# A network of two blocks: the gated unit by seven block products, and the expert stage's start, order of projections and end rearranged

## The reference

```python
def peer_ffn(h, w_q, sub_keys, u, v):            # first block: x = x + peer_ffn(rmsnorm(x, norm_ffn), ...)
    q = (ht @ w_q).reshape(T, PEER_HEADS, 2, PEER_DKEY // 2)                  # 512 tokens, 8 heads, 2 x 128
    s = jnp.einsum('thpc,hpnc->thpn', q, sub_keys)
    v1, i1 = lax.top_k(s[:, :, 0], K)                                          # K = 16
    v2, i2 = lax.top_k(s[:, :, 1], K)
    cand = (v1[..., :, None] + v2[..., None, :]).reshape(T, PEER_HEADS, K * K)
    cand_idx = (i1[..., :, None] * PEER_NKEYS + i2[..., None, :]).reshape(T, PEER_HEADS, K * K)
    top_s, pos = lax.top_k(cand, K)
    idx = jnp.take_along_axis(cand_idx, pos, axis=-1)
    g = jax.nn.softmax(top_s, axis=-1)
    ue = jnp.take(u, ib, axis=0)                                               # 128 tokens at a time
    a = jnp.einsum('thkd,td->thk', ue, xb)
    w = jax.nn.gelu(a) * gb
    ve = jnp.take(v, ib, axis=0)
    return jnp.einsum('thk,thkd->td', w, ve)

# second block, second mixer: the gated unit behind the state-space layer
    z = jax.nn.gelu(y)
    mix = (z @ w_glu_a) * jax.nn.sigmoid(z @ w_glu_b)
    x = x + gate_m * mix
# second block, second feed-forward
    h = _rmsnorm(x, norm_g[layer, 1]) * (1.0 + scale_f) + shift_f
    x = x + gate_f * (jnp.square(jax.nn.relu(h @ w_fc1[layer])) @ w_fc2[layer])
```

## Time and profile before

| What | Value |
|---|---|
| Runs of the kernel | 3541.75, 3543.51, 3547.22 us |
| Profiled execution, its own time | 3536.91 us |
| Its span, first to last instruction | 3535.1 us |
| Mean granted clock of TensorE | 0.958 |
| PE / DVE / ACT / POOL busy | 89% / 56% / 20% / 19% |
| Moved by DMA | 799.12 MB, of it 619.09 MB on the queue of POOL |
| Expert stage, norm to next stage's norm | 628.77 to 1999.99 us |
| Gated unit, first matmul to last root | 2997.44 to 3117.44 us |

### The profile page before, as it was taken

One profiled execution on the slowest core, in us unless ns is written; L12 is line 12 of the kernel. 1 busy time (PEld: TensorE's weight loads), 2 busy tenths in 40 slices (PEclk: granted clock), 3 DMA queues, 4 the chain that ended last, 5 costly groups with the idle time before them and its releaser, 6 DMA issues. The chain is left out here.

```text
span 3535.1 us, 29320 instructions
## 1 busy us (share of the span) xinstructions
PE 3160.9 (89%) x10728; PEld 1644.0 (47%) x10728; DVE 1973.6 (56%) x4299; ACT 710.6 (20%) x1547; POOL 659.2 (19%) x649
## 2 busy tenths in 40 slices
PE   8999799889888777887877889999999978989998
PEld 3454454334333333333333334534444466468887
DVE  5565831477667777777776319435653366056422
ACT  2133221122222222222221220112110033011000
POOL 0110100144445445444444100000000000000000
PEclk9999899999999999899899999999999999999999
DMA  5653411599999999999999322113453354212222
GB/s 194 240 161 108 155 60 60 220 422 417 417 419 407 421 421 421 421 420 421 409 421 421 155 109 84 48 41 115 159 190 136 120 192 171 71 60 84 84 85 82
DMA packets 118672, 799.12 MB, mean 226 GB/s; under 512 B 13728, under 2 KB 16416, under 8 KB 31872
## 3 DMA queue, kind: packets, MB, share of 16 engines
q0 software_dynamic: 91312, 619.09, 43.6%
q1 hardware_dynamic: 27216, 178.15, 14.1%
HBM read 767.83 MB, written 29.36 MB: 226 GB/s over the span
## 5 line engine op out<-in xcount | busy, mean ns | idle before, releaser
L1278 PE MATMUL po<-pair,diag 128*128 128x512 f32 x2048 | 992.5, 643 | 221.0 <-ACT diag L1338 220.9
L1425 DVE SCALAR_TENSOR_TENSOR pair<-pair,h_tm 128x1024 f32<-128x1024 f32 x512 | 616.7, 1225 | 298.5 <-DMA pair<-in_peer_uv,idx 295.0
L1278 PEld LDWEIGHTS po<-pair,diag 128*128 128x128 f32 x2048 | 411.7, 205 | 781.0 <-issue 489.7
L1198 POOL DMA_INDIRECT pair<-in_peer_uv,idx x512 | 586.8, 1146 | 959.5 <-PE po L1278 663.1
L1571 PE MATMUL acc<-a,ring 128*128 128x512 f32 x512 | 220.9, 592 | 0.0
L1332 ACT ACTIVATE ge<-a 128x4 f32<-128x4 f32 x128 | 26.3, 205 | 896.0 <-DVE pair L1425 896.0
L1556 PE MATMUL acc<-hT,ring 128*128 128x512 f32 x480 | 206.2, 592 | 0.0
L1338 ACT ACTIVATE diag<-ident,wt 128x128 f32<-128x128 f32 x512 | 163.7, 390 | 29.5 <-DVE wt L1428 29.5
L1571 PEld LDWEIGHTS acc<-a,ring 128*128 128x128 f32 x512 | 97.3, 190 | 122.5 <-issue 122.5
L1556 PEld LDWEIGHTS acc<-hT,ring 128*128 128x128 f32 x480 | 91.2, 190 | 114.8 <-issue 114.8
L523 PE MATMUL acc<-hT,first 128*128 128x512 f32 x304 | 136.0, 602 | 5.4 <-ACT mg L707 5.4
(11 more groups left out here) (462 smaller groups left out, 4030.6 us busy)
## 6 DMA issues: line engine op xcount, KB each, us to landing
ring<-in_w_fc SPq DMA_DIRECT2D x62, 1024.0 KB, 4.9
mg<-in_ada_w POOLq DMA_DIRECT2D x96, 512.0 KB, 5.0
s_tables<-table POOLq DMA_DIRECT2D x16, 1664.0 KB, 6.6
tab<-s_tables SPq DMA_DIRECT2D x16, 1664.0 KB, 6.4
ring<-in_w SPq DMA_DIRECT2D x15, 1024.0 KB, 4.8
first<-in_w_first SPq DMA_DIRECT2D x14, 1024.0 KB, 5.1
other<-in_w_first SPq DMA_DIRECT2D x14, 1024.0 KB, 5.0
pair<-in_peer_uv,idx POOLq DMA_INDIRECT x512, 14.7
```

What stands on the lines that cost most here:

```text
L1198: pool.indirect_dma_start(out=pair[:, at, :], out_offset=None, in_=core.dram["peer_uv"][:, :], in_offset=bass.IndirectOffsetOnAxis(ap=idx[ ...
L1278: last = pe.matmul(po[:, t % 2, half * 512:(half + 1) * 512], diag[:, at, :], pair[:, at, D + half * 512:D + (half + 1) * 512], start=firs ...
L1425: dve.scalar_tensor_tensor(row, row, 1.0, h_tm[:, t, :], ALU.mult, ALU.mult, accum_out=a[:, g, s:s + 1]).then_inc(dotted, 1)
```

## The change

- Expert stage, start: the norm runs over the first 128 tokens, then over the other 384. The projections 0 and 1 run over the first 128 tokens (`project_first`), unit 0 is scored and tile 0 turned, then the same projections run over the rest (`project_rest`). Then follow score 1, the projections 2 and 3 and score 2. On ACT the exponentials of the units 0 and 1 stand ahead of the projections 2 and 3. The keys and `iota` are loaded ahead of weight chunk 1.
- Expert stage, middle: twelve projections (4 to 15) in the units 0 to 11 (`LAST_PROJECT` 11), each in two halves behind the gathers 4 and 8 of a unit. Groups of gathers (`groups`): two in the units 0 to 11, four after that, and in the last unit 4, 4, 4, 2, 1, 1. `tokens(1)` in unit 0, `tokens(2)` and `tokens(3)` behind the units 12 and 13. The operations over `hit` run once for both halves of the key, with 512 elements; `cand` and `left` share its memory. ACT copies a tile's output behind the first group of the next unit.
- Expert stage, end: tiles are turned back, added, squared and summed one at a time: 0, 1 and 2 within the units 17 to 31, tile 3 at the end.
- Gated unit: `glu_halves`, with the seven products of `Pairs` for the pairs 1 to 7 and whole products (`Pairs.first`) for pair 0; the weights are laid out for it on the host.
- Last feed-forward: its pairs run through `Pairs` too; pair 0 is made of whole products, which follow the norm tile by tile.

```diff
-LAST_PROJECT = 10
+LAST_PROJECT = 11
...
+def groups(unit):
+
+    if unit <= LAST_PROJECT:
+        return [(s, 2) for s in range(0, PK, 2)]
+    if unit < UNITS - 1:
+        return [(s, GRP) for s in range(0, PK, GRP)]
+    return [(0, 4), (4, 4), (8, 4), (12, 2), (14, 1), (15, 1)]
...
-            sp.dma_start(ring[1], w[P:2 * P, :]).then_inc(w_landed[1], 16)
             sp.dma_start(keys[:, :, :], core.dram["sub_keys"].rearrange("p (h n) -> p h n", n=PN)).then_inc(tables, 16)
             sp.dma_start(iota[:, :], core.const("iota16")).then_inc(tables, 16)
+            sp.dma_start(ring[1], w[P:2 * P, :]).then_inc(w_landed[1], 16)
...
         @block.tensor
...
+            def project_first(i):
+
                 for k in range(KT):
                     if i == 0:
-                        pe.wait_ge(products.ready, k + 1)
+                        pe.wait_ge(normed, k + 1)
+                    last = pe.matmul(acc[:, i, 0:P], ring[0][:, k * 256 + i * P:k * 256 + (i + 1) * P], core.hT[:, k, 0:P],
+                                     start=(k == 0), stop=(k == KT - 1))
+                last.then_inc(first_made, 1)
...
+            pe.wait_ge(core.first_landed, 16 * fetched)
+            project_first(0)
+            project_first(1)
             pe.wait_ge(tables, 32)
             score(0)
+            tokens(0)
+            project_rest(0)
+            project_rest(1)
             score(1)
-            tokens(0)
-            project(2)
-            tokens(1)
-            project(3)
+            for i in range(2, 4):
+                project(i, 0)
+                project(i, 1)
             score(2)
-            tokens(2)
-            tokens(3)
-            project(4)
-            project(5)
...
+                if unit == 2 * PH + 2:
+                    turn_back(1)
+                if unit == 2 * PH + 3:
+                    sum_squares(0)
+                    sum_squares(1)
...
+                    end = s0 + size
+                    if unit <= LAST_PROJECT and end in (4, 8):
+                        project(unit + 4, end // 4 - 1)
+                    if end == 12 and unit + AHEAD + 1 < UNITS:
                         score(unit + AHEAD + 1)
-            turn_back(1)
-            for k in range(KT):
-                sums.add(pe, k)
+                    if end == 12 and unit == 0:
+                        tokens(1)
+                    if end == PK and unit in (LAST_PROJECT + 1, LAST_PROJECT + 2):
+                        tokens(unit - LAST_PROJECT + 1)
+                    if end == 8 and unit == UNITS - 1:
+                        turn_back(2)
+            sum_squares(2)
+            turn_back(3)
+            sum_squares(3)
...
         @block.scalar
...
+            for i in range(2):
+                act.wait_ge(first_made, i + 1)
+                act.activation(qT[:, i, 0:P], acc[:, i, 0:P], ACT.Copy).then_inc(first_taken, 1)
             score(0)
+            tokens(0)
+            for i in range(2):
+                act.wait_ge(made, i + 1)
+                act.activation(qT[:, i, P:S], acc[:, i, P:S], ACT.Copy).then_inc(taken, 1)
+            exponentials(0)
             score(1)
-            tokens(0)
+            exponentials(1)
             project(2)
-            tokens(1)
-            exponentials(0)
             project(3)
             score(2)
...
+                    if end == PK and unit == 0:
+                        tokens(1)
...
-                for q in range(2):
-                    step(dve.tensor_tensor(hit[:, :, :], partf[:, q, :].unsqueeze(2).to_broadcast([P, PK, PK]),
-                                           iota[:, :].unsqueeze(1).to_broadcast([P, PK, PK]), ALU.is_equal))
+                step(dve.tensor_tensor(hit[:, :, :, :], partf[:, :, :].unsqueeze(3).to_broadcast([P, 2, PK, PK]),
+                                       iota[:, :].unsqueeze(1).unsqueeze(1).to_broadcast([P, 2, PK, PK]), ALU.is_equal))
...
+class Pairs:
...
+    def first(self, pe, ready=None):
+        for out, column, done in ((self.x(0), 0, self.x_made), (self.y(0), 1, self.made)):
+            for k in range(KT):
+                if ready is not None and column == 0:
+                    pe.wait_ge(ready, k + 1)
+                last = pe.matmul(out, self.halves.block(0, 2 * column + k // 4)(k % 4), self.h[:, k, :], start=(k == 0), stop=(k == KT - 1))
+            last.then_inc(done, 1)
...
+def glu_halves(core, following):
...
+        @block.scalar
+        def _(act):
+            for p in range(KT):
+                if p >= 2:
+                    act.wait_ge(mixed, p - 1)
+                if p:
+                    pairs.copies(act, p)
+                    pairs.first_quarter(act, p, gate[:, p % 2, LOW], ACT.Sigmoid).then_inc(pairs.c_taken, 1)
+                    act.wait_ge(added, p)
+                    sums.square(act, p - 1)
+                    act.wait_ge(pairs.y_taken, p)
+                    act.activation(gate[:, p % 2, HIGH], gate[:, p % 2, HIGH], ACT.Sigmoid).then_inc(gated, 1)
+                else:
+                    act.wait_ge(pairs.x_made, 1)
+                    act.activation(gate[:, 0, :], pairs.x(0), ACT.Sigmoid).then_inc(pairs.x_copied, 1)
...
```

More of the change, by code:

```diff
@@ new lines, in out @@
+            def out(unit):
+                t = place(unit)[0]
+                act.wait_ge(used, (unit + 1) * PK)
+                for half in range(2):
+                    part = slice(half * 512, (half + 1) * 512)
+                    act.activation(y_tm[:, t, part], po[:, t % 2, part], ACT.Copy).then_inc(tile_out, 1)
+            for i in range(2):
+                act.wait_ge(first_made, i + 1)
+                act.activation(qT[:, i, 0:P], acc[:, i, 0:P], ACT.Copy).then_inc(first_taken, 1)
@@ L1414, in _ @@
                 pick_experts(unit)
+            done = 0
             for unit in range(UNITS):
                 t, h = place(unit)
-                if unit < 2 * AHEAD:
+                if h == 0:
                     dve.wait_ge(copied, 2 * t + 2)
-                for g in range(PK // GRP):
-                    for s in range(GRP):
-                        n = unit * PK + g * GRP + s
+                for s0, size in groups(unit):
+                    for s in range(s0, s0 + size):
+                        n = unit * PK + s
                         at, _, filled = slot[n]
@@ L1646, in sum, with wait, block @@
-    def sum(self, c, i, k):
-        return self.sums[:, c % 2, i - 1, k * P:(k + 1) * P]
-def core_first_or_ring(feed, c):
-    return feed.core.first[:, :] if c == 0 else feed.ring[:, (c - 1) % 2, :]
+    def wait(self, pe, c, n):
+        pe.wait_ge(self.ready, 4 * c - 4 + n)
+    def block(self, c, i):
+        w = self.feed.chunk(None, c, False)
+        return lambda k: w[:, i * 512 + k * P:i * 512 + (k + 1) * P]
+    def sum(self, c, i):
+        return lambda k: self.sums[:, c % 2, i - 1, k * P:(k + 1) * P]
@@ L1751, in _ @@
                     if kk == 0 and j == 0:
[L1752 removed]
+                        pe.wait_ge(pairs.y_taken, HT - 1)
                     if kk == 0 and j:
                         pe.wait_ge(added, 2 * j)
[L1755 removed]
+                    quarter(pe, last_half, halves.block(n, 3), lambda k: t[:, 2, at + k, :], start).then_inc(made, 1)
                     if kk == 1 and j:
```

506 lines of the change are left out of this document (271 added, 235 removed).

## The result

The changed kernel takes 3497.56 us (median of four runs, 3497.26 to 3498.12) against 3542.63 for the kernel before in the same comparison: a ratio of 0.9874, 95% interval 0.9858 to 0.989. The forecast was 3508, range 3501 to 3525. The direction was right; the time lies 3.4 us under the range.

The account below looks back on a forecast made before the run. It took the DMA stream to bound the expert stage and TensorE the gated unit and last feed-forward. Terms summed to -35.2 us on the profiled 3536.9, giving 3501.7; plus 6.6 for the median, 3508, range 3501 to 3525.

Parts of the forecast that it names:

- norm to first gather: Expert stage, start: norming and projecting 128 tokens first brings the first gather earlier, minus 10 us.
- dry gap, block 2: Expert stage, unit 0: no dry stream, minus 8 us; weight block 2 now loads inside the stream, plus 2.5 us.
- after the last landing: Expert stage, end: smaller last groups let TensorE finish sooner behind the last gather, minus 5 us.
- gated unit: Gated unit: seven products of 256 columns per pair in place of 32 instructions of 512, minus 9.8 us.
- first pair of the feed-forward: Last feed-forward, start: whole blocks let TensorE follow each biased tile, minus 4.9 us.
- median above the profiled execution: Whole kernel: the median of the runs lies 6.6 us above the profiled execution, added to the sum.
- Start of the stream: Expert stage, start: scoring 9.5 us earlier, merged `hit` operations 0.5 us less, first gather at about 647.0, minus 10 us.
- The dry gap: Expert stage, unit 0: exponentials of unit 1 ahead of the projections keep the stream from running dry, minus 8 us.
- sums of squares of tile 2 (32 instructions of 128 columns, 4.4): Expert stage, end: TensorE work behind its last weights, 4.4 us within a tail of 14.1 us.
- (D): Rival, gated unit: its pairs wait for copies and sums, 3513 us; chance 0.1.
- (B): Rival, expert stage: the stream still runs dry in unit 0, 3516 us, with the slow start 3521; chance 0.2.
- (E): Rival, units 0 to 11: short bursts let TensorE's clock fall, slower, 3575 us at a clock of 0.75; chance 0.04.

Follow-up runs that it names:

- run 11: The changed kernel with groups of four gathers in units 0 to 11 too, in place of two: 3496.16 us, ratio to before 0.9878.
- run 3: The kernel before with only the exponentials of unit 1 moved ahead of tokens(2), tokens(3) and projection 4: 3540.7 us, ratio to before 1.0005.
- run 6: The kernel before with only projections 4 and 5 moved into the units, exponentials left behind tokens(3): 3534.7 us, ratio to before 0.9992.
- run 8: The changed kernel with the norm and first two projections over all 512 tokens before the first scoring: 3503.31 us, ratio to before 0.9905.
- run 1: The changed kernel with the whole expert stage of the kernel before: 3520.8 us, ratio to before 0.9954.
- run 5: The kernel before with projections 4 and 5 moved into the units and the exponentials of unit 1 moved ahead: 3531.8 us, ratio to before 0.9979.
- Run 7: The changed kernel with each matmul of the new sums of squares issued twice: 3498.7 us, ratio to before 0.9888.
- run 4: The changed kernel with the last unit of the expert stage in groups of four: 3503.3 us, ratio to before 0.9901.
- run 14: The changed kernel with groups of four in units 0 to 11, last tile turned back earlier, last unit 4, 4, 2, 2, 2, 1, 1: 3492.04 us.
- run 12: The changed kernel with the last tile turned back before the squares of tile 2 are summed: 3495.9 us, ratio to before 0.9878.
- run 9: The changed kernel with the last feed-forward of the kernel before: 3501.17 us, ratio to before 0.989.

## Why the prediction was right, and where it was wrong

| term | forecast | trace |
|---|---|---|
| stage before the norm (unchanged code) | 0 | +2.8 |
| norm to first gather | -10 | -11.15 |
| dry gap, block 2 | -8 + 2.5 | -7.06 |
| after the last landing | -5 | -10.25 |
| the stages up to the norm at 2807 (unchanged) | 0 | +0.9 |
| gated unit | -9.8 | -9.1 |
| first pair of the feed-forward | -4.9 | -5.0 |
| sum on the profiled execution | -35.2 | -38.8 |
| median above the profiled execution | +6.6 | -0.6 |

**What bounds it**, the stream: right. The share is 1.01 before and after, and run 11 shows that steps in its shade cost nothing.

**Start of the stream**: right within 1.2 us. The first gather came 17.0 us behind the norm (forecast 18.2), since the 32 short instructions took 5.46 us where I had 6.5, and scoring followed TensorE's last of them after 0.46 us where I had 0.7. The last landing came 15.4 us earlier, as forecast (15 to 16), but in part by luck: the stage before, whose code is unchanged, ended 2.8 us later, and the two terms gave 2.7 us more than forecast.

**The dry gap**: the size was near, the cause wrong. I named the exponentials, because the trace put DVE's 14.87 us on them. They were one of two waits. The other, ACT and TensorE on projections 4 and 5, ended 1.5 us later and holds the slot as long by itself, and it also held up the exponentials. My list by hand had the two projections left in front of unit 0 right and so gave the right result for the wrong line: run 3 moves that line alone and gains nothing, run 6 moves the other and gains the gap. Run 8 confirms the 2.5 of block 2 as 2.6. The gap itself is no fixed number: 7 us of idle stream in the trace that the 8 was read from, 4 in runs 1 and 3, where projections 4 and 5 started 3.4 us sooner. Later in the stream it scatters too: first gather to last landing, the same data took 1308.2 us in run 8 and 1310.5 and 1311.2 in runs 5 and 6, all without a gap. What moves it there was not tried.

**After the last landing**: right in mechanism, wrong in size. TensorE ended 6.3 us behind the last landing, 6.1 were forecast. Of the 4.7 us less than before, 1.7 are the half clock that the first trace of before happened to have there (run 1). The step that failed is "sums of squares of tile 2 (32 instructions of 128 columns, 4.4)" and "32 instructions more 4.5": they are 16 each, 1.95 and 2.05 us. That is 4.9 of the 5.3 us; the copies and hand-overs between give the rest. A tile's sum is eight matmuls, and every matmul of this kernel shows as two instructions; I doubled once too often. Run 7 bears the size out: 32 instructions more cost 3.6 us, 0.11 each, where the forecast had 0.14.

**Gated unit and feed-forward**: right, 13.0 forecast and 12.95 measured for a pair with its sum, 4.9 and 5.0 for the first pair. (D) did not happen. The -9.1 is the difference of two traces; from the norm at 2807 to that of the feed-forward the 11 traces with the new unit take 275.5 to 279.3 us and the four others besides before 285.8 to 288.2.

**The median**: the step "The median of the runs is 6.6 above it" is the largest miss. It took the median of three runs for a property of the kernel, and for one that the change leaves alone. Of 56 runs of before only three were above that median of 3543.51. Whether that was luck or the chip of those runs is open; the changed kernel's four runs beside them lay 0.0 to 0.9 us under their own profiled execution. Against the pooled median, 1.4 us above the profiled execution, the same sum gives 3503.1, and with the sums of squares sized by their rows 3498.2, where the pooled median of after is 3497.9. It took both steps to miss: with either one put right, the lower end of the range would lie at 3496, under the result.

**Rivals.** (B): the share stayed at 1.01 in 673 to 715, and slot 12's gather went out at 705.24 (listed: 703.9). (E): the clock was 0.97 in 700 to 1140. The rule of the Trainium skill that spoke for it (TensorE: Matmul & The Clock Gate, HAM oscillation) does not take hold here: TensorE's bursts there are on the whole not shorter than its waits, since it is busy for 392.80 of 440 us.

## What to carry to other kernels

A wait that the trace puts down to one instruction may hide a second that ends at about the same time, and may itself be held up by it: before pricing its removal, list what the waiting chain needs next and when that is ready. Count the instructions of a short step from the rows of its like, not from the loop: here one factor of two was worth as much as a whole term. And with three runs that spread over 5 us, sum and result are best both held against a profiled execution, or against a median of many runs.

## What the hardware showed that I had not expected

Much of the scatter between the profiled executions is the placing of short spells at half clock. From the norm at 2356 to the one at 2807 (times of the changed kernel) the code is unchanged. In the 16 profiled executions of this study that stretch took 450.8 us six times, 452.5 six times and 453.6 or 453.7 four times, and each time the granted clock of its first 15 us or so tells which: never under full speed, half clock for 3.4 us, half clock for 6.8 us. Here are the changed kernel (450.8), run 8 (452.5) and run 4 (453.7), columns as in the earlier trace rows:

```profile
2360.00:2365.00 5.00, 5.00 (x13) 2.27 (x12) 1.62 (x3) 2.38 (x4) 0.00 (x0) 1.00 0.99 401
```
```profile
2360.00:2365.00 5.00, 4.86 (x8) 2.11 (x9) 3.87 (x6) 4.63 (x7) 2.19 (x5) 0.66 0.93 387
```
```profile
2360.00:2365.00 5.00, 2.00 (x3) 1.00 (x4) 3.65 (x6) 3.89 (x7) 3.23 (x6) 0.69 0.56 180
2365.00:2370.00 5.00, 5.00 (x9) 2.10 (x8) 1.73 (x3) 2.49 (x4) 0.05 (x1) 0.62 1.00 406
```

The same holds behind the expert stage. In the changed kernel TensorE, idle for most of 1970 to 1975, gets 0.50 in the 5 us that follow, and its first 32 instructions take 16.84 us; in run 8, after the same wait, it gets 1.00 (1980 to 1985) and they take 13.97. Of the 11 traces with the new end of the expert stage, run 14 and the edits of runs 4, 7 and 12 included, three (runs 7, 8 and 9) take 13.97 and eight 16.6 to 17.0.

```profile
1970.00:1975.00 5.00, 1.45 (x13) 1.26 (x12) 0.70 (x2) 2.07 (x3) 0.00 (x0) 0.91 0.00 0
1975.00:1980.00 5.00, 4.80 (x6) 2.19 (x7) 4.69 (x8) 0.53 (x1) 0.00 (x0) 0.50 0.94 357
```
```profile
1981.07 13.97 PE L1541 MATMUL acc<-hT,first 128*128 128x512 f32 x32 [3.75 <-DVE hT L313]
```

So the same idle time costs 0 or 2.9 us. The Trainium skill, TensorE: Matmul & The Clock Gate, section What's actually happening, says that the gate looks at activity in a rhythm of its own, which does not start anew with the kernel; the traces fit that, with 16.84 and 13.97 us behind the same wait, but no run here shifts a stage by a known amount to show it. In any case unchanged code varies by that much from one execution to the next: over the 16 traces the first two stages behind the expert stage took 88.3 to 91.6 and 288.6 to 293.7 us. This fits runs 7 and 8, whose medians show less than their own stretches.
